# The two split weight tiles begin 16 bytes further in each partition

## What is computed

```python
(gq, gk, gv, ga, gz, dq, dk, dv, iq, ik, iw, dz, xq, xz, gates) = split_cols(h @ w_in[i])
merged = (s_gla * (y_gla @ w_gla_out[i]) + s_dsa * (y_dsa @ w_dsa_out[i]) + s_mem * (y_mem @ w_x_out[i]))
...
mix = jnp.concatenate([main, mo], axis=-1) @ w_out[l]
gate, up = jnp.split(h @ w_in, 2, axis=-1)
return (jax.nn.silu(gate) * up) @ w_out
```

## Time and profile before

| | |
|---|---|
| median of 3 runs | 2001.47 us |
| lowest and highest run | 1994.1 and 2008.78 us |
| profiled execution, span from first to last instruction | 2001.5 us |
| TensorE busy in it | 1968.7 us, 98% |
| weight loads busy | 1781.3 us, 89% |
| VectorE, ScalarE, GpSimd busy | 57%, 47%, 7% |
| matmuls | 13488 |

### The profile page before, as it was taken

One profiled execution on the slowest core, in us unless ns is written; L12 is line 12 of the kernel. 1 busy time (PEld: TensorE's weight loads), 2 busy tenths in 40 slices (PEclk: granted clock), 3 DMA queues, 4 the chain that ended last, 5 costly groups with the idle time before them and its releaser, 6 DMA issues.

```text
span 2001.5 us, 32809 instructions
## 1 busy us (share of the span) xinstructions
PE 1968.7 (98%) x13488; PEld 1781.3 (89%) x13488; DVE 1145.0 (57%) x1595; ACT 932.6 (47%) x1647; POOL 145.5 (7%) x149
## 2 busy tenths in 40 slices
PE   8999999999999999999999999999999999999998
PEld 6798888877889778888999899999988799999998
DVE  3375347465343233353353999972377659999523
ACT  4443142355433342355454755652258856565422
POOL 0000000000000000000000233300000003333000
PEclk9999999999999999999999999999999999999999
DMA  6521122211334123332212233332231113223331
GB/s 179 146 85 64 43 84 84 85 64 59 111 112 162 63 106 105 106 116 89 81 48 80 77 125 106 106 126 95 97 116 43 64 64 116 106 106 106 127 106 64
DMA packets 29824, 191.24 MB, mean 96 GB/s; under 512 B 3689, under 2 KB 4841, under 8 KB 8562
## 3 DMA queue, kind: packets, MB, share of 16 engines
q1 hardware_dynamic: 26562, 178.58, 25.4%
q0 software_dynamic: 3120, 10.62, 2.0%
HBM read 185.38 MB, written 3.67 MB: 94 GB/s over the span
## 4 chain that ended last, share of the span: by engine, by line
PE 90%; DVE 5%; ACT 3%; issue 1%; DMA 1%; SPq 0%; DVEq 0%; ACTq 0%
PE PS L561 21%; PE PS L563 20%; PE PS L562 20%; PE PS L1034 6%; PE PS L1036 6%; PE PS L1035 6%; DVE wlo L2721 1%; ACT whi L1546 1%; PE PS L895 1%; PE PS L714 1%; PE PS L731 1%; PE PS L1152 1%; PE PS L917 1%; PE PS L851 1%; PE PS L1344 1%
## 5 line engine op out<-in xcount | busy, mean ns | idle before, releaser
L2323 DVE TENSOR_TENSOR wlo<-raw,whi 128x2048 fp32r<-128x2048 f32 (+2 forms) x117 | 264.9, 2264 | 375.3 <-ACT whi L1546 374.9
L1546 ACT ACTIVATE whi<-raw 128x2048 fp32r<-128x2048 f32 (+2 forms) x250 | 311.7, 1256 | 211.1 <-PE PS L563 190.7
L561 PE MATMUL PS<-hhi,whi 128*128 128x512 f32 (+1 forms) x768 | 313.2, 408 | 3.1 <-DVE hlo L2370 3.0
L563 PE MATMUL PS<-hhi,wlo 128*128 128x512 f32 (+1 forms) x768 | 302.7, 394 | 0.0
L562 PE MATMUL PS<-hlo,whi 128*128 128x512 f32 (+1 forms) x768 | 301.3, 392 | 0.0
L561 PE MATMUL PS<-whi,ahi 128*128 128x256 f32 x704 | 196.1, 279 | 0.0
L562 PE MATMUL PS<-wlo,ahi 128*128 128x256 f32 x704 | 196.1, 279 | 0.0
L563 PE MATMUL PS<-whi,alo 128*128 128x256 f32 x704 | 196.1, 278 | 0.0
L561 PEld LDWEIGHTS PS<-hhi,whi 128*128 128x128 f32 (+1 forms) x768 | 144.4, 188 | 40.7 <-DVE hlo L2370 5.4
L1034 PE MATMUL PS<-shi,whi 128*128 128x256 f32 x640 | 179.5, 280 | 0.9 <-DVE gated_ L2766 0.4
L1036 PE MATMUL PS<-shi,wlo 128*128 128x256 f32 x640 | 178.5, 279 | 0.0
(11 more groups left out here) (458 smaller groups left out, 4605.8 us busy)
## 6 DMA issues: line engine op xcount, KB each, us to landing
raw<-in_stream SPq DMA_DIRECT2D x165, 1024.0 KB, 4.8
gpost<-in_gposts POOLq DMA_DIRECT2D x5, 512.0 KB, 7.6
X<-in_x SPq DMA_DIRECT2D x4, 512.0 KB, 6.1
X<-in_x POOLq DMA_DIRECT2D x1, 2048.0 KB, 10.4
out<-X SPq DMA_DIRECT2D x4, 512.0 KB, 2.6
bias_line<-linet POOLq DMA_DIRECT2D x1, 1536.0 KB, 35.1
tbias<-bias_line POOLq DMA_DIRECT2D x1, 1024.0 KB, 7.5
memx<-in_mem POOLq DMA_DIRECT2D x1, 1024.0 KB, 5.4
```

Source lines behind the costliest of these rows:

```text
L561: nc.tensor.matmul(out, lh, rh, start=(k == 0), stop=False)
L563: return nc.tensor.matmul(out, ll, rh, start=False, stop=(k == n_k - 1))
L1546: return nc.scalar.activation(out_, in_, func, scale=scale)
L2323: V_.tensor_tensor(wlo[:, s % 2, :, cols_], raw[:, s % 2, :, cols_], whi[:, s % 2, :, cols_], ALU.subtract)\
```

## The change

The two tiles are declared with four more float32 numbers in each partition, and the kernel uses a view of each that leaves the first four out. All shapes, loops and instructions stay.

```diff
+OFF_LINE = 4
...
         raw = sb("raw", [P, 2, KT, C])
-        whi = sb("whi", [P, 2, KT, C], F32R)
-        wlo = sb("wlo", [P, 2, KT, C], F32R)
+        whi, wlo = (sb(name, [P, OFF_LINE + 2 * KT * C], F32R)[:, OFF_LINE:].rearrange("p (s k c) -> p s k c", s=2, k=KT)
+                    for name in ("whi", "wlo"))
```

## The result

The change makes the kernel slower. The median is 2024.13 us (2022.54 to 2026.19, four runs) against 2003.99 us before (1994.1 to 2008.78); the ratio on record is 1.0118, with a 95% interval of 1.0088 to 1.0148, and the two medians alone give 1.010, inside it. The profiled execution has a span of 2022.4 us. The time of a run is about 2 us above its span (2024.51 and 2022.4 us here, 1.7 to 2.2 us in the other runs). So it isn't right that nothing lies around the span: the profiled execution of the kernel before, with 2001.5 us, took about 2003.5 us as a run (an estimate), and the 2001.5 of the forecast's sum met the median of 2001.47 by chance.

A forecast was written before the change was run, and what follows sets the result against it. The prediction took TensorE's split-product matmuls, their number by their pace, to bound the kernel. Instructions, loads, writers and TensorE reads each added 0 to the profiled 2001.5 us, giving 2001 us, with an 8-in-10 range of 1942 to 2046 us.

The forecast's parts named there:

- the slower sign: The outcome that the whole kernel gets slower by over 1%: about 2035 us, tail to 2122, chance 0.25.
- What bounds the kernel: TensorE, 98% busy: the time is the number of split-product matmuls by their pace, and little else.
- the bound of 2 us for the writers: ScalarE writing whi and VectorE writing wlo at shifted starts: taken as 0, bounds -2 and +2 us.
- The other tiles move by 64 bytes, a multiple of all that the rows hint at: 0 us: Loads part: tiles behind the two weight tiles shift by 64 bytes, claimed to cost 0 us.
- I take 0, because the only row with shifted pieces shows 0: Ground for 0 us on TensorE's reads: the unsplit float32 product has shifted moving pieces and pays nothing.
- The term of the reads by TensorE: Cost of TensorE reading split operands from shifted starts: taken as 0 us, bounds -104 and +121 us.
- The start address is not what selects the pace: Second ground for 0 us on TensorE's reads: all operands started 0 bytes off 64, yet both 256-column paces occurred.
- all slow costs 0.25 x 8,736 x 4.45 = 10 us: Case of history re-dealing paces, all 256-column matmuls slow: 10 us, counted within no change, which together had chance 0.42.
- The lower bound of -104 us: TensorE's reads at best: all loss in split matmuls goes, 65.5 us at 256 columns and 38.4 us at 512.
- the 65.5 us: Largest gain on 8,736 matmuls with 256 moving columns, their mean pace going from 116.7 to 109.2 ns.
- The faster rival: Split matmuls' two operand streams fall out of step: 46 us less, about 1955 us, tail to 1898; chance 0.33.
- The slower rival: 256-column runs of whi or wlo need one more 64-byte piece: 34 us, 2035 us, or 78 us, 2079; chance 0.25.

The follow-up runs named there:

- e5_scan: Bare split matmuls in the real layout, distance from weight tile to activation tile scanned 0 to 496 bytes in 16-byte steps; at 64, 256 columns reached 113.3 ns.
- e2_others64: Kernel before the change with padding behind wlo, so only the tiles behind the two weight tiles move by 64 bytes: 2031.31 us, ratio 1.0158.
- e6_all64: Kernel before the change with padding ahead of whi, so weight tiles and all tiles behind move by 64 bytes, distances kept: 2002.49 us, ratio 1.0005.
- e9_only16: The change plus 192 bytes of padding behind, putting activation tiles back at their old place modulo 256: 2019.56 us, ratio 1.0106 against the kernel before.
- e10_width: Bare 512-column split matmuls with weight loads of 128 to 32 columns, four distances, plus unsplit ones; 226.7 and 234.3 ns at 128, 231.6 and 230.6 at 32.
- e8_scan: Bare-matmul distance scan repeated with weight tiles 16, 32 or 48 bytes behind a multiple of 64; in the change's places 234.4, 118.3 and 117.8 ns.
- e7_all16: Kernel before the change with weight tiles and all tiles behind them starting 16 bytes further, distances kept modulo 256: 1988.27 us, ratio 0.9929.
- e13_length: Bare split matmuls with 128 to 512 moving columns, loads of 32 or 128 weight columns, four distances; beside 128, both 128 and 192 columns take 111.7 ns.
- m_c,w_c: Setting in a bare-matmul run: moving tile and weight tile both 32 bytes behind a multiple of 64; 227 ns with 512 columns.
- e1_pairs: Bare matmuls, TensorE alone, moving and weight tiles at various byte offsets; 512 columns take some 227 or 233 ns depending on the pair of places.
- e11_best: All tiles 16 bytes further as in e7_all16, plus feed-forward left operands and the sums behind moved by 128 bytes: 1984.72 us, ratio 0.9912 against the kernel before.

## Why the prediction was wrong

The forecast was no change, 2001 us; measured is 2024.13 us, 1.2% above the kernel before by the ratio. That lies inside the range, but only because the range had been drawn around two rivals of opposite sign; the slower sign had a chance of 0.25, and its mechanism was another.

*What bounds the kernel* was right. The time is the pace of the split matmuls. The growth of their pace, 28 us, is all of the 20.9 us in the spans, and the rest is what the clock hid. No wait, load or writer took part; the bound of 2 us for the writers held with 0.

*"The other tiles move by 64 bytes, a multiple of all that the rows hint at: 0 us"* is the first step that failed. I had read steps of 6.67 ns, 16 columns or 64 bytes, and took 64 for the period. The period of the distance is 256 bytes (e5_scan). This by-effect alone costs 1.6% (e2_others64), and moving all tiles by 64 costs nothing (e6_all64).

*"I take 0, because the only row with shifted pieces shows 0"* is the second. The term of the reads by TensorE, put at 0, was 1.1%, about 20 us, for the 16 bytes alone (e9_only16). The row failed as a witness, at the weakness that was named: the unsplit product moves a column every second cycle. It takes 215.8 ns at every distance tried (e10_width), while split ones take 226.7 to 238.8 (e5_scan, e8_scan). *"The start address is not what selects the pace"* was wrong as a ground. Before the change every pair stood at one setting, 0 and 64, and this setting happens to be one with two paces; that history chooses between the two is no evidence on what another setting does. e7_all16 has the fast one nearly throughout in T. The case *"all slow costs 0.25 x 8,736 x 4.45 = 10 us"*, which I had counted as no change, is a good part of what happened: in the new places T takes 118.1 ns and P 118.3, and almost nothing of the 113.3 is left. From the paces before, 115.8 and 117.3, to 117.8 this makes 5,088 x 2.0 + 3,648 x 0.5 ns = 12 of the 28 us. But it was the addresses that took the fast pace away, not the history.

The lower bound of -104 us was too wide. It let the matmuls with 256 columns reach 109.2 ns, and e13_length shows none below 111.7 beside a load of 128 columns; with that figure the 65.5 us become 8,736 x 5.0 = 44 us.

*The faster rival* named the right variable, the distance between the two operands, with the wrong modulus and with no ground for a sign. Its layout exists, 0.7 to 0.9% faster, but the change doesn't hit it. *The slower rival* had the right sign by a wrong mechanism. An additional piece on operands off a multiple of 64 would slow `m_c,w_c` and e7_all16, which are fast, and would spare the other tiles' shift, which is slow.

The Trainium skill, "SBUF — State Buffer", section "Specifications (TRN2)", has 16-byte cachelines, and I had drawn from it that a whole line costs nothing. The runs contradict that use: at a kept distance 16 bytes change the kernel by 0.7%. The same page of the Trainium skill, section "Who interferes with whom", says that TensorE's two reads are independent and wait for nobody. In the runs the place of the weights changes the pace of the moving operand: with the weights alone moved by 64 bytes, 512 columns take 233.3 ns and not 226.7 (e1_pairs), with no other engine at work. The measurement decides.

What stays open is how the reads get in each other's way. The loss grows with the moving columns, it exists with a load of 32 columns of weights, and unsplit matmuls don't have it; so it seems to belong to the full-rate read of float32r. With a load of 32 columns only the moving tile was moved, so these runs don't show whether the place of the weights still counts there. Whether the two-paced settings can be steered was not tried.

## What to carry to other kernels

A change of a tile's size moves all tiles behind it. Where TensorE bounds the kernel with float32r operands, such a by-effect can be taken for the effect of the change itself: 64 bytes cost 1.6% here, and 16 bytes with all distances kept gained 0.7%; so compare addresses before the source, and hold the rest in place with padding. A scan of bare matmuls over start and distance takes one run. It foretold e9_only16 to 0.5 us and missed e11_best by 6 us; the scan over the distance alone missed e7_all16 by 12 us, 0.6%. A witness that runs at half rate says nothing on full rate. And two profiles are compared at a like granted clock, or its share is taken out first: here it was about 6 us of 27.

## What the runs showed of the hardware

- Float32r matmuls back to back took 226.7 to 238.8 ns with 512 moving columns and 113.3 to 120.3 with 256 in the scans of the real layout, set, in steps of 16 bytes, by the distance of weights and moving operand modulo 256 bytes and the start modulo 32. Unsplit float32 took 215.8 ns for 512 cycles at all four distances tried.
- Beside a load of 128 columns, 128 and 192 moving columns of float32r both took 111.7 ns (e13_length).
- Paces come in steps. The triples of the kernel before take 340.0 or 353.3 ns and 686.7 or 700.0 ns, 13.3 ns apart.
- A setting can have two paces, 113.3 and 117.8 ns in form T at start 0 and distance 64, which hold over long stretches: counted from the starts, 45 of 49 unbroken stretches of 256-column matmuls in the trace of the kernel before kept one pace from end to end, the longest of them over 1,474 matmuls. This can make its spread, 1994 to 2009 us. The clock doesn't: at the same mean clock of 0.997 it took 1993.59 and 2005.07 us. In e7_all16, where T has one pace, two runs at 0.995 took 1985.97 and 1987.12 us, and two at 0.994 1989.42 and 1989.96. No run shows the paces of a slow and a fast execution of the same kernel side by side.
